# First expert products between the gathers, and one low part of x made while the ranks are awaited: a four-layer decoder in float32 on one core

## The reference

```python
def _moe(h, router_w, router_b, w_gate, w_up, w_down):
    hf = h.reshape(bsz * seq, d)
    scores = jax.nn.sigmoid((hf @ router_w).astype(jnp.float32))
    sel = scores + router_b.astype(jnp.float32)
    grp = lax.top_k(sel.reshape(-1, N_GROUPS, EXPERTS_PER_GROUP), 2)[0].sum(-1)
    g_idx = jnp.argmax(grp, axis=-1)
    in_group = (jnp.arange(N_EXPERTS) // EXPERTS_PER_GROUP)[None, :] == g_idx[:, None]
    _, e_idx = lax.top_k(jnp.where(in_group, sel, -jnp.inf), TOP_K)
    w = jnp.take_along_axis(scores, e_idx, axis=-1)
    w = w / jnp.sum(w, axis=-1, keepdims=True)
    ...
    for e in range(N_EXPERTS):
        he = jax.nn.silu(hf @ w_gate[e]) * (hf @ w_up[e])
        y = y + combine[:, e:e + 1] * (he @ w_down[e])
```

## Time and profile before

| | |
|---|---|
| median of 3 runs | 1706.59 us (1705.85 to 1707.25) |
| the profiled execution, its own time | 1708.22 us |
| its span | 1706.4 us |
| PE busy | 1652.1 us, 97% of the span |
| DVE busy | 717.2 us, 42% |
| ACT busy | 466.9 us, 27% |
| DMA, mean over the span | 313 GB/s |
| mean granted clock of TensorE | 0.987 |
| chain that ended last | PE 79%, DVE 11%, DMA 6%, ACT 2% |

### The profile page before, as it was taken

How to read it: one execution, slowest core, us unless ns; L and a number is a source line. 1 busy time by engine, 2 the same in 40 slices (tenths; PEclk the granted TensorE clock), 3 DMA queues, 4 the chain that set the end, 5 groups by cost and what they waited for, 6 DMA issues and landing times.

```text
span 1706.4 us, 18037 instructions
## 1 busy us (share of the span) xinstructions
PE 1652.1 (97%) x7604; PEld 969.3 (57%) x7604; DVE 717.2 (42%) x1052; ACT 466.9 (27%) x549; POOL 48.8 (3%) x47
## 2 busy tenths in 40 slices
PE   7999999999999999999999999999999999999998
PEld 6874433358777843432588777634334887434335
DVE  4572111194657721111856755511115657211117
ACT  5521111044443311110444342211112552111102
POOL 0000000010000000000010000000010000000000
PEclk9989999999999999999999999999999999999999
DMA  7488999955442899999544445999996549899992
GB/s 285 185 358 338 423 421 421 419 220 185 156 178 108 351 422 421 421 421 421 208 174 189 157 174 227 420 421 421 421 420 280 203 188 373 336 422 421 421 413 87
DMA packets 75146, 534.43 MB, mean 313 GB/s; under 512 B 8976, under 2 KB 9136, under 8 KB 10544
## 3 DMA queue, kind: packets, MB, share of 16 engines
q1 hardware_dynamic: 73728, 530.95, 76.6%
q0 software_dynamic: 1328, 2.21, 0.4%
HBM read 532.07 MB, written 1.05 MB: 312 GB/s over the span
## 4 chain that ended last, share of the span: by engine, by line
PE 79%; DVE 11%; DMA 6%; ACT 2%; issue 1%; DVEq 0%; SPq 0%; ACTq 0%
PE psum L957 36%; PE psum L565 9%; PE psum L567 9%; PE psum L566 9%; PE psum L949 4%; DVE w_lo L1453 3%; DMA raw<-in_experts 3%; PE psum L709 3%; PE psum L967 2%; PE psum L576 2%; DMA expert_high<-in_experts 1%; DMA expert_work<-in_experts 1%; PE psum L883 1%; ACT w_hi L1162 1%; PE psum L891 1%
## 5 line engine op out<-in xcount | busy, mean ns | idle before, releaser
L1453 DVE TENSOR_TENSOR w_lo<-raw,w_hi 128x2048 fp32r<-128x2048 f32 x120 | 273.0, 2303 | 156.4 <-ACT w_hi L1162 153.0
L565 PE MATMUL psum<-w_hi,xT_hi 128*128 128x512 f32 x640 | 254.9, 398 | 8.4 <-DVE w_lo L1453 6.7
L567 PE MATMUL psum<-w_hi,xT_lo 128*128 128x512 f32 x640 | 250.0, 391 | 0.0
L566 PE MATMUL psum<-w_lo,xT_hi 128*128 128x512 f32 x640 | 249.9, 390 | 0.0
L1162 ACT ACTIVATE w_hi<-raw 128x2048 fp32r<-128x2048 f32 x120 | 224.2, 1909 | 89.9 <-PE psum L567 85.8
L957 PE MATMUL psum<-raw,xg 128*64 128x512 f32 x864 | 203.0, 597 | 0.2 <-DMA raw<-in_experts 0.2
L1162 ACT ACTIVATE work<-psum 128x512 f32<-128x512 f32 x152 | 89.4, 599 | 409.6 <-PE psum L567 206.9
L565 PEld LDWEIGHTS psum<-w_hi,xT_hi 128*128 128x128 f32 x640 | 120.7, 189 | 38.1 <-issue 7.6
L957 PE MATMUL psum<-expert_work,xg 128*64 128x512 f32 x600 | 139.6, 598 | 1.6 <-DMA expert_work<-in_experts 1.6
L566 PEld LDWEIGHTS psum<-w_lo,xT_hi 128*128 128x128 f32 x640 | 120.8, 189 | 25.7 <-issue 1.2
L567 PEld LDWEIGHTS psum<-w_hi,xT_lo 128*128 128x128 f32 x640 | 120.6, 188 | 25.6
(11 more groups left out here) (165 smaller groups left out, 1611.2 us busy)
## 6 DMA issues: line engine op xcount, KB each, us to landing
raw<-in_experts SPq DMA_DIRECT2D x159, 1024.0 KB, 15.0
raw<-in_slots SPq DMA_DIRECT2D x120, 1024.0 KB, 4.8
expert_work<-in_experts SPq DMA_DIRECT2D x109, 1024.0 KB, 14.6
expert_high<-in_experts SPq DMA_DIRECT2D x64, 1024.0 KB, 12.7
expert_bias<-in_experts SPq DMA_DIRECT2D x24, 1024.0 KB, 11.5
expert_norm<-in_experts SPq DMA_DIRECT2D x20, 1024.0 KB, 13.5
expert_y<-in_experts SPq DMA_DIRECT2D x4, 1024.0 KB, 15.3
expert_xg<-in_experts SPq DMA_DIRECT2D x4, 1024.0 KB, 8.8
```

The source lines that it names most:

```text
L565: mm(out, lhs[0], rhs[0], start=start, stop=False)
L566: mm(out, lhs[0], rhs[1], start=False, stop=False)
L567: return mm(out, lhs[1], rhs[0], start=False, stop=stop)
L1453: return tt(lo, whole, hi.bitcast(F), ALU.subtract)
```

## The change

Three things move. On PE, two gathers of the first quad come first, then the first gate product, the third gather, the second gate product, the fourth gather, and the last two gate products; the read of the flag and the wait for the rest of `pick` stand behind them. The counts for the flag go to bank 0 instead of bank 4, which leaves bank 4 free for the gate products; they wait until ACT has copied tile 0's embedding out of banks 0 and 1. On DVE, the low part of x for the second tile moves from ahead of `route` to the place between `cw` and `key`.

```diff
@@ route, PE
-                mm(psum[:, 4, 0:NE], ones[:, :], chosen[:, 0, :], start=True, stop=False)
-                mm(psum[:, 4, 0:NE], ones[:, :], chosen[:, 1, :], start=False, stop=True
+                pe.wait_ge(emb_ready, 4 * L + 2)
+                mm(psum[:, 0, 0:NE], ones[:, :], chosen[:, 0, :], start=True, stop=False)
+                mm(psum[:, 0, 0:NE], ones[:, :], chosen[:, 1, :], start=False, stop=True
                    ).then_inc(rank_in_psum, 1)
@@ experts, PE
-                for i in range(4):
-                    if i == 3:
-                        pe.wait_ge(xg_ready, 16 * L + 1)
-                    gather(0, i, (5, 6, 7, 5)[i])
+                for i in range(2):
+                    gather(0, i, 5 + i)
+                for s in range(4):
+                    pe.wait_ge(xg_ready, 16 * L + s + 1)
+                    wide(0, "gate", 4, s)
+                    if s < 2:
+                        gather(0, s + 2, (7, 5)[s])
                 pe.wait_ge(flag_ready, L + 1)
                 crowded = pe.value_load(flag[0:1, 0:1], min_val=0, max_val=NE)
                 pe.wait_ge(pick_ready, 2 * T * (L + 1))
-                for s in range(4):
-                    pe.wait_ge(xg_ready, 16 * L + s + 1)
-                    wide(0, "gate", 4, s)
@@ DVE
+            def split_x(L, t):
+                dve.wait_ge(x_hi_ready, T * L + t + 1)
+                rest(x_split[1][:, t, :], x[:, t, :], x_split[0][:, t, :]).then_inc(x_lo_ready, 1)
+
@@ route, DVE
                 step(tt(cw[:, :, :], score[:, :, :], chosen[:, :, :], ALU.mult))
+                split_x(L, 1)
...
-                link(ts(big[:, :], psum[:, 4, 0:NE], HALF + 0.5, None, ALU.is_gt),
+                link(ts(big[:, :], psum[:, 0, 0:NE], HALF + 0.5, None, ALU.is_gt),
@@ the layers' loop, DVE
-                for t in range(T):
-                    dve.wait_ge(x_hi_ready, T * L + t + 1)
-                    rest(x_split[1][:, t, :], x[:, t, :], x_split[0][:, t, :]).then_inc(x_lo_ready, 1)
+                split_x(L, 0)
                 route(L)
```

## The result

The changed kernel takes 1709.84 us, the median of 20 runs (1705.71 to 1714.16); the kernel before took 1706.39 (20 runs, 1703.20 to 1712.01). The ratio is 1.0020, with a 95% interval of 1.0012 to 1.0028: **3.4 us slower, 2.0 to 4.8**. The forecast was 1707.2, no measurable change, with a range up to 1709.6; the median lies 0.2 above it. The mean granted clock of the 20 runs is 0.988, and 0.987 in the runs of the kernel before that stood beside the experiments, so the clock does not explain the loss.

The account below looks back on a forecast made before the run. The prediction took the weight stream to end the expert stages, PE being faster but catching up with the queue. Layers 0 and 3 at 0.33 us each gave +0.65 on the 1706.59 median: 1707.2 us, range 1705.2 to 1709.6.

Parts of the forecast that it names:

- TensorE 0.65 us later: First pair's gathers and gate products on PE: the reordered pieces take 11.75 us instead of 11.10, in every layer.
- (b): Rival: the flag load behind the fourth product is exposed on PE in layers 0 and 3; +5.2 us, 1711.8; chance 0.09.
- (c): Rival: switching between gathers and products is free on PE, so nothing is lost; 0, 1706.6 us; chance 0.12.
- (d): Rival: the first gather's copy arrives late and the first product waits 0.6 us in layers 0 and 3; 1708.4; chance 0.07.
- VectorE: Low part moved between `cw` and `key`: `key` slips at most 0.44 us; 0.2 taken in layers 1 and 2, 0 elsewhere.
- The ninth decides: Weight queue, layer 0: the ninth refill, not the first, sets the queue's end, moving it by up to +0.65 us.
- I take half in layers 0 and 3: Weight queue's end in layers 0 and 3: half the 0.65 us slip counts, 0.33 us each, ends 0 and 0.65.
- Layers 1 and 2: 0: Queues there hold work, so 0.65 + 0.2 us on PE only shortens its waits for weights; cost 0.
- a sign of being wrong: Expert stages: the prediction called itself wrong if, among other signs, layers 1 or 2 changed in length.
- full as well: Weight queue of layer 2 after the rank step: taken as full like layer 1's, from a stretch at 1.01.
- rival a: Early first refills survive, so layers 0 and 3 gain up to 1.95 us each; 3.9 in all, 1702.7; chance 0.10.
- +3.0 if nothing is absorbed anywhere: Upper bound over all four layers: 4 x 0.65 + 0.4 us if no slip on PE or VectorE is absorbed.

Follow-up runs that it names:

- e17_later_dve: Kernel before with the next quad's first two gathers moved later as in e13_later, plus only VectorE's part of the change: 1704.46 us against 1706.96, ratio 0.9985.
- e13_later: Kernel before, next quad's first gather ahead of first pair's last up product, second behind second pair's last gate product: 1703.16 us against 1706.40, ratio 0.9983.
- e9_slip_ninth: Kernel before with three filler products behind the first pair's last up product: 1708.29 us against 1707.72, ratio 1.0008.
- e11_late: Kernel before, next quad's first gather ahead of first pair's last up product, second behind second pair's second gate product: 1706.79 us against 1707.72, ratio 0.9996.
- e1_dve: Changed kernel with TensorE's order of the kernel before, so only VectorE's move and the counts in bank 0: 1707.85 us against 1706.83, ratio 1.0008.
- e10_layer2: Changed kernel with its TensorE order in layer 2 alone, the other layers in the order of before: 1707.55 us, ratio 1.0006.
- e2_pe: Changed kernel without VectorE's move; TensorE's new order and the counts in bank 0 stay: 1710.02 us, ratio 1.0018.
- e15_all_but_2: Changed kernel with its TensorE order in layers 0, 1 and 3, layer 2 in the order of before: 1708.92 us against 1706.40, ratio 1.0017.
- e18_later_pe: Changed kernel without VectorE's move, with the next quad's first two gathers moved later as in e13_later: 1706.73 us, ratio 1.0000.
- e4_slip_double: Kernel before with six filler products between the first pair's second and third product: 1712.15 us, ratio 1.0030.
- e5: Changed kernel with the first quad as two gathers, two products, two gathers, two products: 1710.14 us against 1707.26, ratio 1.0009.
- e12: As e11_late, with the first quad as two gathers, two products, two gathers, two products: 1706.77 us, ratio 0.9997.
- e14: As e13_later, with the first quad as two gathers, two products, two gathers, two products: 1706.20 us, ratio 1.0001.
- e16: Whole changed kernel with the next quad's first two gathers moved later as in e13_later: 1706.04 us, ratio 1.0000.

## Why the prediction was wrong

**TensorE 0.65 us later: right** (0.69). So were its pieces: the copy of the first gather was there, the flag load hid, and the refills went out where the steps said, 4.1, 7.1, 14.8 and 27.7 us behind the gather. The four products ended 0.69 us later, with no idle time between the pieces, where by the rule of the Trainium skill (TensorE: Matmul & The Clock Gate, section Part 2) the added changes of kind would be free. Here the measurement decides against it. Rivals (b), (c) and (d) did not come.

**VectorE: its size was wrong in layer 2, at no cost that can be seen.** I took `key` to slip by at most 0.44 us in layers 1 and 2, from layer 1's wait. By the traces it slipped by 0.04 in layer 1 and 0.56 in layer 2. Timeline of VectorE in layer 2 of the changed kernel:

```profile
1085.71 1.22 DVE L1454 TENSOR_TENSOR work_r<-x,work_r 128x1024 fp32r<-128x1024 f32 x1
1086.85 0.18 DVE L1762 SCALAR_TENSOR_TENSOR key<-psum,chosen 128x32 f32<-128x32 f32 x1
```

TensorE's first gather came 2.3 us behind its first rank product there and 1.9 before, and TensorE waited 1.19 us for the picks instead of 0.63. From layer 1's last product to layer 2's first gather it is 276.3 us before and 276.4 after, so the stretch did not get longer, and e17_later_dve is level with e13_later (0.9985 and 0.9983). This is outside the stage in any case.

**"The ninth decides": half right.** e9_slip_ninth, with the eighth and later ones 0.9 us late, lost 1.4 us (-0.2 to 3.1), and 1.3 in layer 2; the same slip of all from the third on lost 4.1. e13_later against e11_late shows that the ninth and those behind it have a large part.

**"I take half in layers 0 and 3": too little for layer 3.** Three profiles of each order in each layer (before, e1_dve, e10_layer2 against after, e2_pe, e15_all_but_2) give means of 209.0 and 209.4 in layer 0 and 208.6 and 209.7 in layer 3: 0.4 and 1.1 us, where 0.33 each was taken. Single profiles of one order differ by up to 0.9 us there, so the 0.4 isn't resolved, and it may be too little: the 70th refill of layer 0 landed 1.6 us later after than before (187.9 and 186.3 us behind the first gather), and only then did the one profile of before lose 1.2 us, between its 74th and 75th refill, that the changed kernel's did not.

**"Layers 1 and 2: 0": this is the step that failed.** Layer 1 is right: 211.3 and 211.1. Layer 2 went from 207.7 in the mean (before, e1_dve, e15_all_but_2: 207.4 to 208.1) to 209.8 (after, e2_pe, e10_layer2: 209.6 to 209.9), 2.1 us. The four differences, 0.4, -0.2, 2.1 and 1.1, add up to the 3.4 that the runs show; with three profiles of each order that close a match is in part luck, and the times of e10_layer2 and e15_all_but_2 give layer 2 less. That layer 2 got longer, which the prediction had named as a sign of being wrong, all six profiles show. I had called the queue of layer 2 "full as well", from a stretch 5 us behind the first gather. It was, there. At the ninth refill, 22 us later, it was not: that load landed 6.7 us after its issue, as layer 0's did (6.6), and not after 9.2 as layer 1's ninth. Already its first refill landed after 7.9, where layer 1's took 10.4. I had read both numbers, 6.7 and 7.9, before I wrote, and used neither. Even 6.7 says too much. A load raises its semaphore in 16 steps, which the trace holds one by one, and 6.7 is the last of them. The median step of the ninth came 5.2 us behind the issue, where it is 4.6 for the first refill of layer 0, into an empty queue. From the ninth load to the tenth the median step takes 3.0 us in the changed kernel and 2.5 before, and against the first gather the tenth's is 1.6 us later. The 1.1 us of waits of the earlier trace rows were no spare either. The stage ends 1.98 us behind the last landing, so a stream that ends later makes these waits and the stage longer (2.3).

**The early refills** (rival a) gave nothing back. Where a first refill is early the next ones follow in 3.0 us (4.08, 7.10), more than the 2.49 that a load lasts, and the second landed 4.8 us after its issue in layer 0, as into an empty queue (4.9). The share at 148 to 150 has fallen to 0.46.

Counting layer 2 like layers 0 and 3 would not have been enough: 3 x 0.33 = +1.0. The prediction's "+3.0 if nothing is absorbed anywhere" is near the measured 3.4 (2.0 to 4.8), but by luck. It takes 0.85 us in each of layers 1 and 2, and they show -0.2 and 2.1. So a second step failed besides the zero for layer 2: the prediction let a layer lose at most what its refills slip (0.65), and layer 2 lost three times that.

**Open.** Why the stream loses more than the slip (2.1 for 0.69 in layer 2). Which of the refills from the third on count. How the loss is shared between layer 2 and layers 0 and 3. And why the level of e18_later_pe is 2.9 us above e13_later, by their ratios, when the stages of its one profile are only 0.8 us longer in sum (834.8 against 834.0); that profile ran 2.0 us under its median.

## What to carry to other kernels

Where a queue is refilled by the engine that it feeds, ask for the time from issue to landing at several loads of each stage, not only whether the first stretch is full. Here a slip of 0.69 us cost 0.4 to 2.1 us in the layers where the ninth load landed 6.6 to 7.0 us after its issue, against 4.9 in an empty queue, and nothing that can be seen where it took 9.2. So don't count a delay ahead of such a load as absorbed; it may cost more than itself. Here it was better to take work out of that stretch and put it where the queue is deeper. Ask too what the end of a stage waits for: here it was the last load's landing, in 79 of 80. And compare stages from a fixed event inside them: layer 2 read 207.4 us in six profiles whose spans differed by 5 us.

## What the runs showed of the hardware beyond that

**A stream near empty moves less while its engines look busy.** In the changed kernel's layer 2 the share is 0.98 and the rate 371 GB/s, where 1.01 goes with 420. No run here shows why.

**The clock can fall in the first quad, and what it costs depends on the queue.** The table by stretches of e17_later_dve, the first 6 us behind the first gather of layer 2, and of e1_dve, the same in layer 1:

```profile
1086.60:1092.60 6.00, 6.00 (x28) 6.00 (x29) 2.82 (x9) 1.67 (x3) 0.00 (x0) 0.51 1.01 421
```

```profile
600.09:606.00 5.91, 5.91 (x27) 5.91 (x28) 2.81 (x9) 1.58 (x3) 0.00 (x0) 0.50 1.02 424
```

The granted clock is 0.5, 1.2 GHz, and the first four products end 2.6 us late in both. Layer 2 is then 210.1 us instead of 207.4 and has lost all of it; layer 1 is 211.2 as ever. It is much like the fillers, made by the chip. In layer 2 it was seen in one of nine profiles of kernels without VectorE's move (e4_slip_double, half as long) and in five of eleven with it (e5, e12, e14, e16, e17), where TensorE had waited 1.19 us for the picks instead of 0.63. Over all eighty stages of the twenty profiles, a wait of 1.19 stands ahead of eleven, all in layers 1 and 2 of kernels with VectorE's move; seven of these have the clock at 0.5 for the whole 6 us, and one at 0.74. Of the other 69 none has it down for the whole 6 us and four for about half of them (0.72 to 0.76). So the move goes with the full fall in these profiles; what that costs in the mean isn't settled, as the times of e17_later_dve show no cost of it.

**A product behind another kind of work costs more than its time.** Six fillers of 0.23 us (1.40) delayed the products by 1.5, and three by 0.9; a group of eight products took 1.87 alone and 1.72 in a row, a group of eight gathers 1.15 and 0.98.
